# Moving sixteen conditioning loads out of a state-space stage and into the weight ring of the feed-forward product

## The chip, the cores and the metric

The kernel runs on one core of one Trainium2 chip. The metric is the device time of one execution in microseconds (us); for the kernel before the change the median of three runs is 3346.17 us (3345.36 to 3350.89). The engines of the core are TensorE (PE in the profile, its weight loads PEld), VectorE (DVE), ScalarE (ACT), GpSimd (POOL) and SyncE (SP, which here only issues transfers). Everything is 32-bit floating point.

## The reference, cut to what matters

A transformer-like stack on 256 tokens of 2048 channels. The first block mixes tokens with a state-space model (S5) whose input is modulated by a conditioning vector, gates the result with a product of 2048 x 4096 (GLU), and then runs an MLP of 2048 x 8192 x 2048 with a squared ReLU. Only the last six lines matter here:

```
sh1, sc1, gt1, sh2, sc2, gt2 = split(silu(c) @ w_mod + b_mod, 6)     # w_mod: 2048 x 12288
h     = rmsnorm(x) * (1 + sc1) + sh1;   y = s5(h) -> GLU
x     = x + gt1 * rmsnorm(y)
h     = rmsnorm(x) * (1 + sc2) + sh2
x     = x + gt2 * rmsnorm(relu(h @ w_mlp_in)**2 @ w_mlp_out)         # gt2 is needed only here
```

The six vectors of 2048 cost a read of 100 MB of `w_mod`, of which each number is used once (the context's own shift and scale come from the same columns). `gt2` is the second branch's gate. After this block come a second block with convolution, spatial gating and two gated FFNs, which the change doesn't touch.

## The kernel before, in words

**Units and the ring.** Every big matrix passes through `raw`, four slots of 1 MB (`[128, 4, 512]` each: four tiles of 128 rows by 512 columns). One such slot is a unit, four units (one slot each) are a block of 512 output columns. In the products of the later stages ACT rounds a unit to fp32r into `w_hi` (`split_unit`, L764), DVE takes the rest `w_lo = raw - w_hi` (L1014, which counts `lo_ready`), SP loads the slot again as soon as `lo_ready` says that its unit is split (L386), and PE multiplies `w_hi` with 512 columns (high and low part of the activations side by side) and `w_lo` with 256 (L478, L479). A block gathers in four of the eight PSUM banks, in turn the lower (`half` 0, banks 0 to 3) and the upper four. DVE folds the halves of a finished block together (L1020, which counts `folded`) after the splits of the next block, and a block may start when the block two before it is folded.

**The conditioning.** `w_mod` passes through the same slots in the state-space stage. There a unit is not split: PE takes it as it lies, 4 matmuls with a stationary tile of 32 columns cut from `cond`, four column groups at a time (`ada_rows`, L1601), and counts `ada_unit`. Of the 24 blocks (96 units) eight hold the first branch's shift and scale (`MOD`, blocks 0 to 3, 6, 8, 10, 12 in loading order) and are needed while the stage runs; the other sixteen (`ADA`) hold gt1, sh2, sc2 and gt2 and are turned into columns once, at the stage's end (`ada_columns`). The stage must be done with all of them before its last step, since DVE then adds the bias (`ada_done`), and the GLU's weights need the slots.

**The state-space stage** is a pipeline over 16 channel tiles, one round each, counted k = -1 to 15. PE's round k begins with the lag blocks of tile k+1 (L1660), then its states (L1676), the outputs of tile k (L1690, L1693), two units of an ADA block, small products for tiles k+2 and k+3 (L1626, L1592, L1634), output transposes (L1703), half the transposes of tile k+2 (L1647), the block's other two units, the other half of the transposes, and in rounds 0 to 3 all four units of one MOD block. Tile k+1's lag blocks wait for powers of C that POOL makes (`powers_of_c`, L2254, `cpow`; `phases` writes `pt` in between), for ACT's copies, and its outputs for a trip of the lag rows through memory (`rw` to `r_scratch` to `tw`, issued by SP). ACT issues most of the `w_mod` transfers (L1491 in `ada_units`), each after a wait until PE has used what lay in the slot; they stand in ACT's queue between its copies.

**The order** of all this is written out by hand: five instruction streams, one per engine, with semaphores between them. No scheduler moves anything.

The lines that the change and the prediction's steps touch: `block_` of GEMM_PE (a block of the products), `unit`/`block_` of GEMM_SP (SP's loads), `split` and `hidden` of GEMM_ACT, `up`/`down` of GEMM_DVE, and the three loops over k.

## Time and profile before

| what | value |
|---|---|
| median of three runs | 3346.17 us (3345.36 to 3350.89) |
| the profiled execution, its own time | 3354.33 us |
| its span on the core | 3352.5 us |
| mean granted TensorE clock | 0.967 of 2.4 GHz |
| state-space stage, up to the first matmul of the GLU | 469.4 us |
| one block of the MLP's product (four units) | 22.19 us |

The profiled execution is one run of the same program. A span is what lies between its first and last instruction; the 1.8 us around it belong to no engine. "Busy" adds up durations of an engine's instructions. A timeline row is a group of like instructions in a row on one engine: its start, its length, the line of the kernel, what it writes and reads, how many, and in brackets how long the engine had been idle before and for whom it waited. fp32 matmuls are recorded twice each, so "x16" of L1601 are 8 matmuls, which are two units. A windows row gives for each engine the busy time in a stretch, the granted clock (PEclk, 1.00 is 2.4 GHz), the busy share of the 16 DMA engines and the rate.

### The profile page before, as it was taken

What the parts mean: (1) busy time and instruction counts of PE and PEld (TensorE: products, weight loads), DVE (VectorE), ACT (ScalarE), POOL (GpSimd) and SP (SyncE); (2) the same over time, 40 slices, a digit from 0 to 9 for tenths busy, and PEclk for the clock granted to TensorE, in tenths of its full rate; (3) what the DMA queues carried; (4) which work ended last, traced back from release to release, by engine and by line L of the source; (5) the groups of instructions that cost most, each with busy time, mean ns of one, the idle gap of its engine ahead of it and who ended that gap; (6) DMA issues with size and microseconds to landing.
All of it is one profiled execution on the core that took longest, in us unless ns stands there. A gap on an engine that the chain in (4) does not pass through costs nothing.

```text
span 3352.5 us, 54116 instructions
## 1 busy us (share of the span) xinstructions
PE 3161.3 (94%) x22461; PEld 2758.8 (82%) x22461; DVE 2139.8 (64%) x1890; ACT 1431.0 (43%) x1559; POOL 324.8 (10%) x227
## 2 busy tenths in 40 slices
PE   5777789899999999899799999999989999999998
PEld 3445568888888888899798888888989888888888
DVE  7668755775555656879666655666555666566565
ACT  4446644433333334376344434433334443443343
POOL 2978730000000000000000000000000000000000
PEclk7789989999999999999899999999999999999999
DMA  9998885555555565465155565555535555556552
GB/s 296 289 306 244 254 276 179 164 164 188 188 188 188 190 191 178 144 201 194 64 182 186 185 200 189 190 192 180 197 111 169 192 191 191 189 178 205 190 188 88
DMA packets 351053, 643.59 MB, mean 192 GB/s; under 512 B 21599, under 2 KB 50359, under 8 KB 350519
## 3 DMA queue, kind: packets, MB, share of 16 engines
q1 hardware_dynamic: 309952, 561.42, 51.6%
q10 hardware_dynamic: 40951, 79.98, 7.2%
q8 instruction: 116, 1.90, 0.2%
q14 instruction: 34, 0.28, 0.0%
HBM read 637.29 MB, written 4.06 MB: 191 GB/s over the span
## 4 chain that ended last, share of the span: by engine, by line
PE 85%; DVE 5%; DMA 4%; ACT 3%; issue 1%; POOL 1%; SPq 1%; ACTq 0%; DVEq 0%; POOLq 0%
PE acc L478 42%; PE acc L479 26%; PE acc L475 5%; PE acc L476 5%; DMA raw<-in_w_mod_dram 3%; PE acc L1601 1%; ACT u L1855 1%; PE acc L1693 1%; PE acc L1676 1%; POOL cpow L2254 1%; DVE w_lo L1014 1%; DMA r_scratch<-rw 1%; DMA tw<-r_scratch 1%; DVE hf L1136 0%; PE acc L1660 0%
## 5 line engine op out<-in xcount | busy, mean ns | idle before, releaser
L1014 DVE TENSOR_TENSOR w_lo<-raw,w_hi 128x2048 fp32r<-128x2048 f32 x484 | 1105.0, 2292 | 908.3 <-ACT w_hi L764 906.6
L764 ACT ACTIVATE w_hi<-raw 128x2048 fp32r<-128x2048 f32 x484 | 923.3, 1914 | 1093.6 <-PE acc L479 1093.3
L478 PE MATMUL acc<-hid,w_hi 128*128 128x512 f32 x3776 | 1309.9, 392 | 0.0
L479 PE MATMUL acc<-xin,w_lo 128*128 128x256 f32 x3968 | 1115.3, 281 | 0.0
L479 PE MATMUL acc<-hid,w_lo 128*128 128x256 f32 x3840 | 1075.0, 280 | 0.0
L478 PE MATMUL acc<-xin,w_hi 128*128 128x512 f32 x2496 | 872.3, 394 | 6.6 <-DVE xin L1126 6.6
L478 PEld LDWEIGHTS acc<-hid,w_hi 128*128 128x128 f32 x3776 | 709.1, 188 | 156.0
L479 PEld LDWEIGHTS acc<-xin,w_lo 128*128 128x128 f32 x3968 | 750.2, 189 | 0.0
L479 PEld LDWEIGHTS acc<-hid,w_lo 128*128 128x128 f32 x3840 | 721.3, 188 | 0.1
L478 PEld LDWEIGHTS acc<-xin,w_hi 128*128 128x128 f32 x2496 | 471.6, 189 | 111.8 <-DVE xin L1126 5.3
L475 PE MATMUL acc<-xin,w_hi 128*128 128x256 f32 x1472 | 415.0, 282 | 4.1 <-DVE xin L1128 2.2
L476 PE MATMUL acc<-xin,w_hi 128*128 128x256 f32 x1472 | 413.9, 281 | 0.0
L475 PEld LDWEIGHTS acc<-xin,w_hi 128*128 128x128 f32 x1472 | 278.8, 189 | 5.9 <-issue 3.2
L476 PEld LDWEIGHTS acc<-xin,w_hi 128*128 128x128 f32 x1472 | 278.7, 189 | 0.0
L1020 DVE TENSOR_REDUCE tmp<-acc 128x1024 f32<-128x2048 f32 x98 | 223.8, 2284 | 0.0
L1601 PE MATMUL acc<-raw,cond 128*32 128x512 f32 x768 | 116.3, 714 | 53.1 <-DMA raw<-in_w_mod_dram 51.1
L1601 PEld LDWEIGHTS acc<-raw,cond 128*32 128x32 f32 x768 | 20.7, 121 | 115.8 <-DMA raw<-in_w_mod_dram 80.0
L838 ACT ACTIVATE xin<-tmp 128x1024 f32 x22 | 23.3, 1060 | 158.0 <-DVE tmp L1266 158.0
L2254 POOL TENSOR_TENSOR cpow<-cpow,ptmp 128x1024 f32<-128x1024 f32 x32 | 75.6, 2362 | 1.3
L1855 ACT ACTIVATE u<-acc,modt 128x32 f32<-128x32 f32 x256 | 70.6, 414 | 1.0 <-PE acc L1634 0.6
L1476 POOL MEMSET conv_in<- 128x120 f32 x1 | 0.2, 203 | 727.6 <-DVE xr L1114 727.6
L2254 POOL TENSOR_TENSOR ptmp<-ct,lpc 128x1024 f32<-128x1024 f32 x32 | 61.9, 1934 | 76.7 <-ACT ct L1793 55.5
(306 smaller groups left out, 2171.1 us busy)
## 6 DMA issues: line engine op xcount, KB each, us to landing
raw<-in_ffn_w_gate_dram SPq DMA_DIRECT2D x88, 1024.0 KB, 5.2
raw<-in_ffn_w_up_dram SPq DMA_DIRECT2D x88, 1024.0 KB, 5.2
raw<-in_ffn_w_down_dram SPq DMA_DIRECT2D x88, 1024.0 KB, 5.2
raw<-in_w_mod_dram ACTq DMA_DIRECT2D x76, 1024.0 KB, 10.1
raw<-in_w_mlp_in_dram SPq DMA_DIRECT2D x64, 1024.0 KB, 5.3
raw<-in_w_mlp_out_dram SPq DMA_DIRECT2D x64, 1024.0 KB, 5.2
raw<-in_s_w_glu_dram SPq DMA_DIRECT2D x32, 1024.0 KB, 5.4
raw<-in_ab_w_in_dram SPq DMA_DIRECT2D x32, 1024.0 KB, 5.5
```

Source lines behind the costliest of these rows:

```text
L475: pe.matmul(bank[:, 0:TOK], w_hi[:, slot, w], operand[:, kt, 0:TOK], start=first, stop=False)
L476: pe.matmul(bank[:, 0:TOK], w_hi[:, slot, w], operand[:, kt, TOK:2 * TOK], start=False, stop=False)
L478: pe.matmul(bank, w_hi[:, slot, w], operand[:, kt, :], start=first, stop=False)
L479: ins = pe.matmul(bank[:, 0:TOK], w_lo[:, slot, w], operand[:, kt, 0:TOK], start=False, stop=last)
L764: act.activation(w_hi[:, slot, :], raw[:, slot, :, :].rearrange("p k n -> p (k n)"), ACT.Copy).then_inc(hi_ready, 1)
L1014: dve.tensor_tensor(w_lo[:, slot, :], raw[:, slot, :, :].rearrange("p k n -> p (k n)"), w_hi[:, slot, :].bitcast(F32), SUB).then_inc(lo_re ...
L1020: dve.tensor_reduce(dst, acc[:, 4 * half:4 * half + 4, :].rearrange("p a (t b) -> p a b t", t=2), AX.X, ADD).then_inc(folded, 1)
L1601: ins = pe.matmul(ps[0][32 * q:32 * q + 32, :], cond[:, kk * UK + q, window:window + 32], raw[:, kk, q, :], start=(m + kk == 0), stop=(kk ...
L1676: ins = pe.matmul(ps[1 + ri][s * NST:(s + 1) * NST, cb * 64:(cb + 1) * 64], ew[:, ri, cb, s * NST:(s + 1) * NST], uv[:, :, ::-1] if d else ...
L1693: ins = pe.matmul(o, st[s * NST:(s + 1) * NST, ri, 4 * d + kp, :], cpow[cp][s * NST:(s + 1) * NST, ri, 4 * d + kp, :], start=False, stop=( ...
L1855: ins = act.activation(u[b][:, g, q * NCH:(q + 1) * NCH], ps[6][:, g * 64 + q * NCH:g * 64 + (q + 1) * NCH], ACT.Identity, bias=modt[:, 16 ...
L2254: return pool.tensor_tensor(o, x, y, op)
```

## The change

Four of the sixteen ADA blocks (gt2, 16 units, 16.8 MB) no longer pass through `raw` in the state-space stage. They pass through the ring in the first part of the MLP, one after every second block of its first eight. Stage by stage:

- State-space stage: 20 blocks instead of 24. MOD blocks are now 0 to 6 and 8 in loading order. The ADA blocks are PE's work in rounds 3 to 14 (12 of them) and no longer in rounds -1 to 14 (16). So round -1 has no unit, rounds 0 to 2 have the four of a MOD block, round 3 has eight (ADA and MOD), rounds 4 to 14 have four as before.
- SP: after the eight loads of an even and an odd block of the MLP come four loads of `w_mod` (`late_gate`), each waiting for the split of the odd block's unit in its slot. The loads of the next block wait until PE has used the late units (`ada_unit`).
- PE: in an odd block, after its first unit, the late units 0 and 1, and after its second the units 2 and 3 (`late_rows`, 32 columns of `ada` broadcast as the stationary tile, into bank 0); after the third unit four small matmuls that turn the row into columns (`late_columns`). Before the first late unit PE waits for the fold of the block before, since bank 0 belongs to it.
- ACT: two small copies per late block, between the splits of the next block (`split_and_turn`).
- DVE: the gate's bias and norm weight are applied in two small instructions in the last part of the MLP.
- The first eight blocks of the MLP are written out and no longer part of a loop on PE and SP; the last three of four parts remain loops.

```diff
-        MOD = [(0, 1), (2, 3), (6, 8), (10, 12)]
-        ADA = [4, 5, 7, 9, 11] + list(range(13, 24))
+        MOD = [(0, 1), (2, 3), (4, 5), (6, 8)]
+        ADA = [7] + list(range(9, 20))
+        ADA_ROUND = 3
...
-                if k + 1 < KT:
-                    if k in (-1, 2, 4):
-                        pe.wait_ge(ada_sb, {-1: 2, 2: 3, 4: 4}[k])
-                    ada_rows(ADA[k + 1], 15 - (k + 1), (0, 1))
+                if k in (-1, 2, 4):
+                    pe.wait_ge(ada_sb, {-1: 2, 2: 3, 4: 4}[k])
+                if ADA_ROUND <= k < KT - 1:
+                    ada_rows(ADA[k - ADA_ROUND], 15 - (k - ADA_ROUND), (0, 1))
...
+            def late_gate(i, u):
+                for k in range(UK):
+                    sp.wait_ge(lo_ready, u + k + 1)
+                    sp.dma_start(raw[:, k, :, :], w_mod[:, k * UK:(k + 1) * UK, 2 * D + (KT - LATE + i) * UN:2 * D + (KT - LATE + i + 1) * UN]
+                                 ).then_inc(raw_ready[k], 16)
...
-            with sp.Fori(0, MLP_PARTS) as q:
+            for c in range(2 * NCK):
+                block_(MLP[0] + 4 * c, *((w_in, c * UN, 0) if c < NCK else (w_out, (c - NCK) * UN, 0)), late=c // 2)
+                if c % 2:
+                    late_gate(c // 2, MLP[0] + 4 * c)
+            with sp.Fori(1, MLP_PARTS) as q:
...
+                    if late is not None and k < 2:
+                        if k == 0:
+                            pe.wait_ge(folded, blk)
+                        late_rows(late, blk - MLP[1], (2 * k, 2 * k + 1))
+                    if late is not None and k == 2:
+                        late_columns(late)
...
+            def late_rows(i, c, units):
+                for kk in units:
+                    pe.wait_ge(raw_ready[kk], 16 * (ADA_UNITS // SLOTS + MLP[0] // SLOTS + c + 1 + i + 1))
+                    for q in range(UK):
+                        kt = KT * 3 + kk * UK + q
+                        ins = pe.matmul(ps[0][32 * q:32 * q + 32, :], ada[:, kt:kt + 1].broadcast_to([P, 32]), raw[:, kk, q, :],
+                                        start=(kk == 0), stop=(kk == UK - 1), skip_group_check=True)
+                    ins.then_inc(ada_unit, 1)
+
+            def late_columns(i):
+                pe.wait_ge(ada_sb, 5 + i + 1)
+                for r in range(NT):
+                    ins = pe.matmul(ps[1][:, r:r + 1], rs[:, r // 2, r % 2 * P:(r % 2 + 1) * P], one_of_32, start=True, stop=True)
+                ins.then_inc(ada_col, 1)
...
+            def split_and_turn(grp, i):
+
+                split(grp, slots=(0, 1), late=i + 1)
+                act.wait_ge(ada_unit, ADA_UNITS + 4 * (i + 1))
+                act.activation(rs[:, :, :].rearrange("p a t -> p (a t)"), ps[0], ACT.Copy).then_inc(ada_sb, 1)
+                split(grp, slots=(2,), late=i + 1)
+                act.wait_ge(ada_col, 5 + i + 1)
+                act.activation(coef[:, 2 * KT + NT * i:2 * KT + NT * (i + 1)], ps[1][:, 0:NT], ACT.Copy).then_inc(ada_done, 1)
+                split(grp, slots=(3,), late=i + 1)
...
+            dve.wait_ge(ada_done, 1 + LATE)
+            x_step(dve.tensor_tensor(gate, gate, par[:, 3 * KT:4 * KT], ADD))
+            x_step.settle()
+            x_step(dve.tensor_tensor(gate, gate, par[:, cols["mlp_post"]:cols["mlp_post"] + KT], MUL))
+            x_step.settle()
```

**PE, round 1 of the state-space stage.** The end of round 1, from the last outputs of tile 1 to the first lag blocks of tile 3, in the kernel before (matmuls counted once each here; `cpow` carries a buffer number):

```order
L1693 MATMUL acc<-cpow_64,st 32x128 x16
L1601 MATMUL acc<-raw,cond 32x512 x8
L1626 MATMUL acc<-mrhs,s5c 128x32
L1592 MATMUL acc<-s5c,craw 64x64 x8
L1634 MATMUL acc<-consts,xt 128x64 x8
L1703 MATMUL acc<-s5c,zt 128x32 x8
L1647 MATMUL acc<-consts,bpow 128x128 x8
L1601 MATMUL acc<-raw,cond 32x512 x8
L1647 MATMUL acc<-consts,bpow 128x128 x8
L1601 MATMUL acc<-raw,cond 32x512 x16
L1660 MATMUL acc<-cpow_63,bd 32x128 x16
```

The same stretch after the change (L1662 is `ada_rows`, L1708 the transposes, L1721 the lag blocks):

```order
L1754 MATMUL acc<-cpow_64,st 32x128 x16
L1687 MATMUL acc<-mrhs,s5c 128x32
L1653 MATMUL acc<-s5c,craw 64x64 x8
L1695 MATMUL acc<-consts,xt 128x64 x8
L1764 MATMUL acc<-s5c,zt 128x32 x8
L1708 MATMUL acc<-consts,bpow 128x128 x16
L1662 MATMUL acc<-raw,cond 32x512 x16
L1721 MATMUL acc<-cpow_63,bd 32x128 x16
```

Both pairs of units in the middle of the round are gone; the four units of the MOD block stay at its end.

**PE, the MLP's second block.** The seam between its first and second unit after the change (with the semaphores that an instruction waits for):

```order
L492 MATMUL acc<-xin,w_hi 128x512
L493 MATMUL acc<-xin,w_lo 128x256
L512 MATMUL acc<-raw,ada 32x512 [waits raw_ready0,folded]
L512 MATMUL acc<-raw,ada 32x512 x3
L512 MATMUL acc<-raw,ada 32x512 [waits raw_ready1]
L512 MATMUL acc<-raw,ada 32x512 x3
L492 MATMUL acc<-xin,w_hi 128x512 [waits lo_ready,xin_ready]
L493 MATMUL acc<-xin,w_lo 128x256
```

Before, the pair L478, L479 of the first unit was followed at once by the first pair of the second; now two late units and a wait for `folded` stand between.

**SP, the loads of the MLP's first part** after the change (before, they were two loops of `w_mlp_in` and `w_mlp_out` loads alone, each waiting for `lo_ready`):

```order
L390 DMA raw<-in_w_mlp_in_dram 128x4x512 [waits lo_ready] x8
L399 DMA raw<-in_w_mod_dram 128x4x512 [waits lo_ready] x4
L390 DMA raw<-in_w_mlp_in_dram 128x4x512 [waits lo_ready,ada_unit] x8
L399 DMA raw<-in_w_mod_dram 128x4x512 [waits lo_ready] x4
L390 DMA raw<-in_w_mlp_out_dram 128x4x512 [waits lo_ready,ada_unit] x8
```

Each set of four late loads sits between blocks, and the loads behind it in SP's queue now also wait for PE's late matmuls.

## Rows read from the trace of the kernel before

**Rows 1.** The page: PE and DMA in 40 slices of 83.8 us (tenths).
```profile
PE   5777789899999999899799999999989999999998
DMA  9998885555555565465155565555535555556552
```

**Rows 2.** Windows: rounds 0 to 3, rounds 4 to 13, one MLP block.
```profile
core 0: us, PE busy (x) PEld busy (x) DVE busy (x) ACT busy (x) POOL busy (x), PEclk, DMA share, GB/s
767.19:789.38 22.19, 22.19 (x130) 19.54 (x129) 13.78 (x7) 8.62 (x5) 0.00 (x0) 1.00 0.57 190
...
109.42:141.95 32.53, 23.16 (x298) 12.72 (x302) 18.37 (x35) 13.63 (x40) 31.66 (x25) 0.77 0.96 281
141.95:170.51 28.56, 23.63 (x302) 12.97 (x298) 16.60 (x32) 13.07 (x40) 28.10 (x20) 0.80 0.94 314
170.51:202.58 32.07, 23.37 (x310) 12.76 (x306) 16.61 (x32) 13.64 (x42) 31.39 (x21) 0.82 0.99 331
202.58:232.28 29.70, 22.16 (x302) 12.46 (x298) 17.18 (x36) 13.07 (x40) 21.71 (x15) 0.84 0.89 287
232.28:442.06 209.78, 165.83 (x2656) 113.51 (x2648) 169.54 (x324) 128.05 (x392) 163.93 (x103) 0.93 0.86 255
```

**Rows 3.** Timeline of PE: starts of rounds 0, 2 and what ended round 1.
```profile
109.42 1.35 PE L1660 MATMUL acc<-cpow,bd 128*32 128x128 f32 x32 [4.35 <-POOL cpow L2254]
...
163.09 1.07 PE L1601 MATMUL acc<-raw,cond 128*32 128x512 f32 x8 [2.23 <-DMA raw<-in_w_mod_dram]
165.86 1.94 PE L1601 MATMUL acc<-raw,cond 128*32 128x512 f32 x8 [1.70 <-DMA raw<-in_w_mod_dram]
168.80 1.93 PE L1601 MATMUL acc<-raw,cond 128*32 128x512 f32 x8 [1.01 <-DMA raw<-in_w_mod_dram]
170.51 1.55 PE L1660 MATMUL acc<-cpow,bd 128*32 128x128 f32 x32
```

**Rows 4.** Timeline of POOL: the last powers for tiles 1, 2, 3, 4.
```profile
107.02 2.34 POOL L2254 TENSOR_TENSOR cpow<-cpow,ptmp 128x1024 f32<-128x1024 f32 x1
...
138.73 2.35 POOL L2254 TENSOR_TENSOR cpow<-cpow,ptmp 128x1024 f32<-128x1024 f32 x1
...
158.00 2.37 POOL L2254 TENSOR_TENSOR cpow<-cpow,ptmp 128x1024 f32<-128x1024 f32 x1
...
177.29 2.38 POOL L2254 TENSOR_TENSOR cpow<-cpow,ptmp 128x1024 f32<-128x1024 f32 x1
```

**Rows 5.** Timeline of PE in a round at full clock, and round 11's start and end.
```profile
179.24 1.06 PE L1612 MATMUL acc<-s5c,adarow 128*128 128x4 f32 x8
180.16 0.39 PE L1626 MATMUL acc<-mrhs,s5c 128*128 128x32 f32 x2
...
305.34 1.92 PE L1601 MATMUL acc<-raw,cond 128*32 128x512 f32 x16
307.19 0.41 PE L1626 MATMUL acc<-mrhs,s5c 128*128 128x32 f32 x2
...
360.45 1.08 PE L1660 MATMUL acc<-cpow,bd 128*32 128x128 f32 x32 [1.57 <-ACT acc L1816]
...
378.77 1.08 PE L1660 MATMUL acc<-cpow,bd 128*32 128x128 f32 x32 [1.62 <-ACT acc L1816]
```

**Rows 6.** Timeline of ACT in the MLP: splits that wait for the end of a unit.
```profile
789.53 1.92 ACT L764 ACTIVATE w_hi<-raw 128x2048 fp32r<-128x2048 f32 x1 [3.69 <-PE acc L479]
795.02 1.92 ACT L764 ACTIVATE w_hi<-raw 128x2048 fp32r<-128x2048 f32 x1 [3.57 <-PE acc L479]
```

**Rows 7.** Timeline of DVE there: the last split of a block, then the fold.
```profile
791.48 2.29 DVE L1014 TENSOR_TENSOR w_lo<-raw,w_hi 128x2048 fp32r<-128x2048 f32 x1 [3.31 <-ACT w_hi L764]
793.69 2.28 DVE L1020 TENSOR_REDUCE tmp<-acc 128x1024 f32<-128x2048 f32 x1
```

**Rows 8.** The page, DMA issues: KB each, median us from issue to landing.
```profile
raw<-in_w_mod_dram ACTq DMA_DIRECT2D x76, 1024.0 KB, 10.1
raw<-in_w_mlp_in_dram SPq DMA_DIRECT2D x64, 1024.0 KB, 5.3
```

More of the change, by code:

```diff
@@ L53, in main_consts @@
     c[:, 2 * P + 7] = 1.0
+    c[::32, 2 * P + 15] = 1.0
     return c
@@ L380, in GEMM_SP, with unit @@
         def GEMM_SP(sp):
-            def unit(u, slot, src, k, col, early=None):
+            def unit(u, slot, src, k, col, early=None, late=0):
+                if late:
+                    sp.wait_ge(ada_unit, ADA_UNITS + 4 * (late - 1) + slot + 1)
                 if early is not None and early < SLOTS:
@@ L404, in GEMM_SP @@
                 glu(i)
-            with sp.Fori(0, MLP_PARTS) as q:
+            for c in range(2 * NCK):
[3 more added lines that the diff above has]
+            with sp.Fori(1, MLP_PARTS) as q:
                 with sp.Fori(0, 4) as i:
-                    block_(32 * q + (4 * i + MLP[0]), w_in, q * (4 * UN) + i * UN)
+                    block_(32 * q + (4 * i + MLP[0]), w_in, q * (4 * UN) + i * UN, late=LATE)
                 with sp.Fori(0, 4) as i:
@@ L455, in GEMM_PE, with block_ @@
         def GEMM_PE(pe):
-            def block_(u, blk, half, operand, ready=None, units=4, slot0=0, between=None, after=1, order=None, narrow=False, piece=None):
+            def block_(u, blk, half, operand, ready=None, units=4, slot0=0, between=None, after=1, order=None, narrow=False, piece=None, late=None):
                 if not isinstance(blk, int):
@@ L704, in down @@
                         block_(32 * q + (8 * i + (MLP[0] + 16 + 4 * j)), 8 * q + (2 * i + (MLP[1] + 4 + j)), j, hid, hid_from(4 * q))
-            for c in range(NCK):
-                block_(MLP[0] + 4 * c, MLP[1] + c, c % 2, xin, normed_from(0), piece=first_from(0) if c == 0 else None)
-            down(0)
+            for c in range(2 * NCK):
+                if c and c % 2 == 0:
+                    pe.wait_ge(ada_done, 1 + c // 2)
+                block_(MLP[0] + 4 * c, MLP[1] + c, c % 2, *((xin, normed_from(0)) if c < NCK else (hid, hid_from(0))),
+                       piece=first_from(0) if c == 0 else None, late=c // 2 if c % 2 else None)
+            pe.wait_ge(ada_done, 1 + LATE)
             with pe.Fori(1, MLP_PARTS - 1) as q:
@@ L766, in GEMM_ACT, with split @@
             ADA_DMA = ADA_UNITS // SLOTS
-            def split(grp, early=False, slots=range(SLOTS)):
+            def split(grp, early=False, slots=range(SLOTS), late=LATE):
                 for slot in slots:
-                    split_unit(4 * grp + slot, slot, 16 * grp + 16 * (ADA_DMA + 1), early)
+                    split_unit(4 * grp + slot, slot, 16 * grp + 16 * (ADA_DMA + late + 1), early)
+            def split_and_turn(grp, i):
[6 more added lines that the diff above has]
+                split(grp, slots=(3,), late=i + 1)
             def weigh(n, c):
@@ L794, in seam @@
                     for grp in left:
-                        split(grp, slots=(SLOTS - 1,))
+                        split(grp, slots=(SLOTS - 1,), late=LATE * s.n)
                     act.wait_ge(x_ms, s.n + 1)
@@ L882, in GEMM_ACT @@
                 for g in (2 * i + 1, 2 * i + 2):
-                    split(g, slots=(0, 1) if g < 8 else (0,))
+                    split(g, slots=(0, 1) if g < 8 else (0,), late=0)
                     if g in (3, 4):
@@ L890, in GEMM_ACT @@
                         weigh(0, 0)
-                        split(g, slots=(2,))
+                        split(g, slots=(2,), late=0)
                         weigh(0, 1)
-                        split(g, slots=(3,))
+                        split(g, slots=(3,), late=0)
                         break
                     if g < 8:
-                        split(g, slots=(2, 3))
+                        split(g, slots=(2, 3), late=0)
                 if i < 3:
@@ L900, in GEMM_ACT @@
             weigh(0, NCK - 2)
-            split(8, slots=(0, 1, 2))
+            split(8, slots=(0, 1, 2), late=0)
             act.wait_ge(pe_unit, 32)
@@ L912, in up @@
                         hidden(4 * q + (2 * i + j), 2 * i + j, j, hid)
-            with act.Fori(0, MLP_PARTS - 1) as q:
+            for c in range(2 * NCK):
+                if c % 2:
+                    split_and_turn(G + 1 + c, c // 2)
+                else:
+                    split(G + 1 + c, late=c // 2)
+                if c < NCK:
+                    hidden(c, c, c % 2, hid)
+            with act.Fori(1, MLP_PARTS - 1) as q:
                 up(q)
@@ L1358, in GEMM_DVE @@
             up(MLP_PARTS - 1)
+            gate = coef[:, 2 * KT:3 * KT]
+            dve.wait_ge(ada_done, 1 + LATE)
[3 more added lines that the diff above has]
+            x_step.settle()
             down(MLP_PARTS - 1, 0, 0)
@@ L1933, in _ @@
                     copy_e(k + 2)
[L1934 removed]
+                if ADA_ROUND <= k < KT - 2:
+                    ada_units(act, ADA[k - ADA_ROUND] + 1, (2, 3))
                 if k + 3 < KT:
```

30 lines of the change are left out of this document (16 added, 14 removed).

## The prediction

> **What bounds the kernel now.** I read the page's slices first. From the seventh slice on PE is busy nine tenths or more in nearly every slice and the DMA engines are at about half; in the first six PE has gaps and the DMA engines stand at eight or nine tenths [rows 1]. So the change takes transfers from where they are scarce and puts them where there is room, but it also takes PE work from where PE has gaps and puts it where PE has none. The time is the difference of two terms, and each needs its own reading.
>
> Next I cut the state-space stage into rounds, from one start of the lag blocks to the next [rows 2]. Rounds 0 to 3, with eight units each, take 32.53, 28.56, 32.07 and 29.70 us at a DMA share of 0.89 to 0.99. Rounds 4 to 13, with four units, take 209.78 / 10 = 20.98 us each at 0.86. The reader is to see that four more units cost about 9 us per round, and that only rounds -1 to 3 can change: from round 4 on the same four units per round stand at the same place in the new program.
>
> Then I asked which wait ends last in each early round. In round 1 PE comes to the four MOD units and waits for three of them one after the other (2.23, 1.70, 1.01 us idle), and right behind them the next lag blocks start without a wait [rows 3]: the loads set the end. But round 0 starts on POOL (PE idle 4.35 us for `cpow`), so POOL is a second clock beside the loads. Its powers for tile 1 end at 107.02 + 2.34 = 109.36, for tile 2 at 141.08, for tile 3 at 160.37, for tile 4 at 179.67 [rows 4]; POOL has no gap between (busy 31.66 of 32.53 and 28.10 of 28.56 us [rows 2]). These are times before which the lag blocks of tiles 2, 3 and 4 cannot start, whatever the loads do.
>
> **The state-space term.** Round -1 loses four units, but its end waits for POOL at 109.36 before and after, and what POOL works from (tables and first modulation) comes from blocks 0 and 1, which are loaded as before: 0 gained. If that cover went, PE's 3.7 us for these units would come free.
>
> Round 0: from 8 to 4 units, but tile 2's powers end at 141.08, and its lag blocks started at 141.95. Gained 0.87 us. That is the step most easily overlooked: this round of 32.53 us was bound twice, and POOL's one-time scaling of powers lies in it.
>
> Rounds 1 and 2: four units each, like a later round. Two floors: POOL makes a tile in 19.29 us (160.37 - 141.08), and the best later round takes 378.77 - 360.45 = 18.32 us [rows 5]. The average is 20.98 us at a granted clock of 0.93 [rows 2], with its dips and late lag rows in it. The MOD units stand at the round's end in one piece (two pairs of 1.85 us), behind both halves of the transposes, so PE can no longer fill its wait for ACT's copies in the middle; on the other hand the first pair no longer delays the small products. I see no reason for better or worse than the average and take 20.9: lag blocks of tile 4 at 141.1 + 41.8 = 182.9, against 202.58. Floor: 179.7 by POOL. Upper bound: the rounds stay at 24 us (the slowest later ones), 189.1.
>
> Round 3 has eight units, as before: 29.70 us then; the three rounds not tied to POOL average 30.1. I take 29.8, from 28.6 to 32.1. Tile 5's lag blocks at 212.7 against 232.28: gained 19.6 us, and between 232.28 - (189.1 + 32.1) = 11 and 232.28 - (179.7 + 28.6) = 24. POOL, 8 us ahead or more by then, is not late in round 4: tile 6 is ready at 179.67 + 2 x 19.29 = 218.3, wanted at 233. The later rounds keep their length, so the gain reaches the GLU. At the stage's end DVE has a shorter add and one 16-column copy more: 0, give or take 0.2.
>
> **The MLP term.** PE is busy 22.19 of 22.19 us in a block at clock 1.00, a unit is 5.55 us [rows 2], so what PE gets there is paid in full.
>
> Late units: in the state-space stage at full clock two units take 307.19 - 305.34 = 1.85 us until the next matmul starts [rows 5], same stationary width, same 512 columns. Four gates of two such pairs: 8 x 1.85 = 14.8 us.
>
> Columns: four matmuls of the same size but 4 columns took 180.16 - 179.24 = 0.92 us [rows 5]; four gates: 3.7 us.
>
> The wait for the fold: bank 0 is free when the block before is folded. DVE folds after the last split: a unit ends at 789.5 (ACT's split starts on it) and the next at 795.0 [rows 6]; the fold runs from 793.69 to 795.97 [rows 7]. PE comes to the late units at 795.0 and waits 0.95 us, 1.05 with the hand-over. This holds in the up and the down blocks alike, since both fold after four splits: 4 x 1.05 = 4.2 us. Behind the waiting matmul PE's whole product is queued. It could be 0 if DVE were early, 2.3 (a whole fold) if something held DVE.
>
> Switching: 16 changes between the 128-wide and the 32-wide tiles. In the trace the next matmul starts 0.07 us before the 32-wide group's recorded end. I take nothing beyond the 1.85. Upper bound: one matmul of 0.39 us drained at each, 6.2 us. The Trainium skill, "TensorEngine Tiling (Array Packing)", section Key Properties, says that changing the tiling mode drains TensorE. The trace neither shows such a cost as a gap nor excludes that it lies inside the 1.85; by that rule read at its dearest the term would be the upper bound, and the time 6 us above my forecast.
>
> The ring: between the use of a late unit and the split of the next block's unit in that slot there must be time to load. Slot 0 is free about 2 us after the odd block's first unit, lands 5.3 us later [rows 8] (8 to 10 if crowded), is split for 4.2 us (1.92 on ACT, 2.29 on DVE), and is wanted three units, 16.6 us and more, after that first unit: 4 to 9 us of room. Slot 2 frees some 10 us after it and is wanted two units later than slot 0: the same. In a late block eight units pass in about 28 us; a ring block shows a share of 0.57 for four in 22.19 us, 3.2 us each, so 25 of 28 us. Tight, not over. Cost 0; if the cover is gone, a unit (5.5 us) per gate.
>
> ACT gets 0.6 + 0.2 us per gate in idle time of 3.6 us per unit, DVE two tiny instructions in the last part within 3.3 us of idle time: 0. SP's waits: 0. Sixteen fewer issues on ACT in the state-space stage are in its rounds already.
>
> Sum: 14.8 + 3.7 + 4.2 = 22.7, and 0.3 for the semaphores inside: +23.0, from 18.5 (no fold wait) to 29.5 (drain).
>
> **The sum.** -19.6 + 23.0 = +3.4 us. Against the profiled execution, 3354.33 + 3.4 = 3357.7; that execution was 8.2 us above the median, so for the median 3346.17 + 3.4 = 3349.6. A difference under 0.2% (6.7 us) can't be told from none.
>
> **Rivals.**
>
> *Faster: all early rounds fall, round 0 and 3 too.* Mechanism: POOL's 141.08 is itself late only because its inputs or its memory accesses are held up by the crowded transfers, and the lighter traffic shortens round 3. Then four rounds give 30.7 - 20.98 = 9.7 us each, 39 us less the eight-unit round that remains (9): 30 us. Time 3346.2 - 30 + 23 = 3339. For it: share 0.96 in round 0. Against: POOL's instructions last the same in crowded and light rounds (2.34 to 2.38 us) and it had no idle time. It decides if tile 2's lag blocks start before 139.
>
> *Slower: rounds 1 and 2 don't fall.* The MOD block's four loads are issued by ACT when PE has used the block before, at the end of a round, and are wanted at the end of the next; with the trip of the lag rows through memory they could keep a round at 25 us. Gain 20 - 2 x 4 = 11 or less, cost 23 to 25: +13, 3359. For it: loads need 10.1 us to land under traffic [rows 8]. Against: they have a whole round. It decides if these rounds are over 24 us.
>
> *Slower: the ring starves behind the late units.* Each gate costs one unit more: +3.4 + 22 = +25, 3372. For it: 25 of 28 us. Against: the slack above. It would show as PE idle for `lo_ready` in the MLP's blocks 2, 4, 6, 8.
>
> *The drain is paid*: +3.4 + 6.2, 3356.
>
> **Chances.** Forecast (within -3 and +9, 3343 to 3355) 0.56; faster rival 0.15; rounds stay 0.14; ring 0.06; drain 0.09. The range leaves out the ring and half the dearest and cheapest cases: 3337 to 3361. Faster by over 0.2%: 0.16 (the rival and the forecast's best edge). Slower by over 0.2%: the two slower rivals, half the drain's, and a little of the forecast's upper edge, 0.27. The same: 0.57.
>
> **What would show it.** Lag blocks of tile 1 at 109.4 again, of tile 2 at 141.1 on a POOL wait; rounds 1 and 2 at 20 to 22 us, round 3 at 29 to 31; GLU's first matmul at about 450. In the MLP, odd blocks of the first part at 22.19 + 5.7 = 27.9 us with PE idle 1 us before the late matmuls for DVE's fold, even blocks at 22.2; two late units at 1.85 us. It is wrong if round 0 shortens by more than 2 us, if an odd block costs over 7 us more, or if an even block is longer.

## The result and the profile after

| kernel | median | spread, runs |
|---|---|---|
| before, beside it | 3348.66 us | 3340.09 to 3353.72, 20 |
| after | 3359.44 us | 3348.78 to 3363.76, 20 |

The ratio is 1.0034, with a 95% interval from 1.0027 to 1.0041: the change costs about 11 us. The forecast was +3.4. The profiled executions differ by less, 3354.33 and 3359.15 us; why is shown with the second profiles of both. Medians below leave out one execution of the kernel with all four late units behind the second unit, which took 11031.7 us at a mean granted clock of 0.339.

The page after, against [rows 1] (40 slices of 83.9 us, in tenths):

```profile
PE   5688789899999999999799999999989999999998
DMA  9588975376656565465255565555534555556552
```

The reader is to see the second slice: DMA falls from 9 to 5 there. In the ninth to eleventh, where the late units now are, it stands at 7, 6 and 6, where it was 5.

Windows of the kernel after: rounds 0 to 3, rounds 4 to 13, an odd and an even block of the MLP's first part. They answer to [rows 2].

```profile
core 0: us, PE busy (x) PEld busy (x) DVE busy (x) ACT busy (x) POOL busy (x), PEclk, DMA share, GB/s
108.96:140.65 31.69, 20.89 (x267) 14.70 (x267) 19.00 (x35) 13.19 (x40) 30.90 (x24) 0.72 0.46 141
140.65:164.98 24.33, 21.02 (x266) 14.48 (x270) 16.60 (x32) 12.57 (x39) 23.87 (x17) 0.67 0.33 94
164.98:186.11 21.13, 19.72 (x278) 14.23 (x274) 16.61 (x32) 13.76 (x42) 20.67 (x15) 0.76 0.80 240
186.11:218.34 32.23, 23.08 (x302) 12.42 (x298) 22.37 (x36) 13.48 (x40) 31.55 (x19) 0.84 0.99 307
218.34:422.94 204.60, 163.31 (x2656) 113.05 (x2648) 168.88 (x324) 127.93 (x392) 169.80 (x108) 0.93 0.89 264
683.59:711.90 28.31, 27.27 (x170) 21.24 (x169) 13.83 (x9) 9.26 (x7) 0.00 (x0) 1.00 0.92 328
711.90:734.08 22.18, 22.18 (x130) 19.52 (x129) 13.81 (x8) 8.62 (x5) 0.00 (x0) 1.00 0.57 190
```

Two things stand here. The DMA engines are at 0.46 and 0.33 in rounds 0 and 1, and at 0.99 in round 3: the loads are spread unevenly. And an odd block is 6.12 us longer than an even one (28.31 against 22.19), although DMA is at 0.92 only and the clock is full.

What sets the early rounds, on PE's timeline; it answers to [rows 3]:

```profile
140.65 1.93 PE L1721 MATMUL acc<-cpow,bd 128*32 128x128 f32 x32 [8.93 <-POOL cpow L2319]
...
157.65 1.94 PE L1708 MATMUL acc<-consts,bpow 128*128 128x128 f32 x8 [2.52 <-ACT ew L1887]
159.52 5.64 PE L1662 MATMUL acc<-raw,cond 128*32 128x512 f32 x32
...
201.90 1.97 PE L1708 MATMUL acc<-consts,bpow 128*128 128x128 f32 x8 [3.60 <-DVE bpow L2015]
...
213.93 1.14 PE L1662 MATMUL acc<-raw,cond 128*32 128x512 f32 x8 [2.48 <-DMA raw<-in_w_mod_dram]
216.64 1.93 PE L1662 MATMUL acc<-raw,cond 128*32 128x512 f32 x8 [1.57 <-DMA raw<-in_w_mod_dram]
```

Round 0 ends with PE idle 8.93 us for POOL's powers; in round 1 no load is waited for, but the four MOD units take 5.64 us, where two pairs at full clock take 2 x 1.85 = 3.7 [rows 5]; of rounds 0 to 3 only round 3 still waits for `w_mod`.

The late units of the MLP's second block (PE) and the folds around it (DVE; [rows 7] before):

```profile
684.60 0.28 PE L493 MATMUL acc<-xin,w_lo 128*128 128x256 f32 x1
685.93 1.92 PE L512 MATMUL acc<-raw,ada 128*32 128x512 f32 x16 [1.04 <-DVE tmp L1075]
687.78 0.50 PE L492 MATMUL acc<-xin,w_hi 128*128 128x512 f32 x1
...
693.32 0.28 PE L493 MATMUL acc<-xin,w_lo 128*128 128x256 f32 x1
693.53 1.92 PE L512 MATMUL acc<-raw,ada 128*32 128x512 f32 x16
695.38 0.50 PE L492 MATMUL acc<-xin,w_hi 128*128 128x512 f32 x1
...
701.03 0.95 PE L519 MATMUL acc<-consts,rs 128*128 128x1 f32 x8
701.85 0.48 PE L492 MATMUL acc<-xin,w_hi 128*128 128x512 f32 x1
```
```profile
683.59 2.28 DVE L1075 TENSOR_REDUCE tmp<-acc 128x1024 f32<-128x2048 f32 x1
...
711.90 2.28 DVE L1075 TENSOR_REDUCE tmp<-acc 128x1024 f32<-128x2048 f32 x1
```

The folds of the two blocks start 28.31 us apart. In steady work a w_lo matmul starts 0.12 us before the next w_hi one. So the first late group starts 685.93 - 684.72 = 1.21 us late, the two groups take 1.85 each, the columns 0.82, and the rest of the 6.12, 0.4 us, lies in small pieces at the switches (0.50 or 0.48 us for the first w_hi matmul behind each group instead of 0.39, and 0.09 us ahead of the second late group).

### The profile page after: what moved, and what is told of

It is laid out like the page before. It is cut to its first block, busy times and chain, and to the rows that moved or that the text cites. A ratio compares the mean times of both kernels' runs of the same rounds, so it can differ in the third digit from the quotient of the medians.

```text
span 3357.2 us, 54092 instructions
## 1 busy us (share of the span) xinstructions
PE 3166.6 (94%) x22493; PEld 2768.6 (82%) x22493; DVE 2145.3 (64%) x1892; ACT 1434.5 (43%) x1567; POOL 324.7 (10%) x227
## 4 chain that ended last, share of the span: by engine, by line
PE 84%; DVE 5%; DMA 3%; ACT 3%; POOL 2%; issue 2%; SPq 1%; ACTq 0%; DVEq 0%; POOLq 0%
PE acc L492 42%; PE acc L493 26%; PE acc L489 5%; PE acc L490 5%; DMA raw<-in_w_mod_dram 1%; PE acc L1662 1%; POOL cpow L2319 1%; DMA tw<-r_scratch 1%; DMA r_scratch<-rw 1%; ACT u L1916 1%; PE acc L1754 1%; POOL ptmp L2319 1%; ACT w_hi L802 1%; DVE w_lo L1069 1%; DVE tmp L1075 1%
## 5 line engine op out<-in xcount | busy, mean ns | idle before, releaser
L1662 PE MATMUL acc<-raw,cond 128*32 128x512 f32 x640 | 94.3, 712 | 27.4 <-DMA raw<-in_w_mod_dram 27.4
L886 ACT ACTIVATE xin<-tmp 128x1024 f32 x22 | 23.3, 1061 | 158.0 <-DVE tmp L1321 158.0
L1662 PEld LDWEIGHTS acc<-raw,cond 128*32 128x32 f32 x640 | 18.4, 124 | 79.2 <-DMA raw<-in_w_mod_dram 42.2
L900 ACT ACTIVATE tmp<-tmp 128x1024 f32<-128x1024 f32 x22 | 23.3, 1061 | 107.2 <-DVE tmp L1314 107.2
```

Source lines behind the costliest of these rows:

```text
L886: act.activation(dst[:, ds(CH * chunk, CH) if not isinstance(chunk, int) else slice(CH * chunk, CH * (chunk + 1)), 0:TOK], tmp[:, half], A ...
L1662: ins = pe.matmul(ps[0][32 * q:32 * q + 32, :], cond[:, kk * UK + q, window:window + 32], raw[:, kk, q, :], start=(m + kk == 0), stop=(kk ...
```

## The experiments

What had to be told apart: is the miss in the stage (less gained than the 19.6 us of the forecast), in the MLP (a late block costs more than 5.75 us), or was the execution profiled before a poor base? And within each part, what sets the price?

**The stage's part alone.** The second branch's gate is taken from its bias alone; its sixteen units are neither loaded nor multiplied anywhere.

```diff
-        ADA_UNITS, LATE = 32 + 3 * KT, KT // 4
+        ADA_UNITS, LATE = 32 + 3 * KT, 0
...
-                    late_gate(c // 2, MLP[0] + 4 * c)
...
-            x_step(dve.tensor_tensor(gate, gate, par[:, 3 * KT:4 * KT], ADD))
+            x_step(dve.tensor_tensor(gate, par[:, 2 * KT:3 * KT], par[:, 3 * KT:4 * KT], ADD))
```

> The changed kernel without any late unit: no loads, no late matmuls, no waits for them in the MLP (left out of the computation: the second branch's gate, 16 units of w_mod). It is the state-space part of the change alone. Theory A (the two terms as the profiles of the pair show them: the stage gives 18 to 21 us, four gates take 24.5): 3348.7 - 19 = about 3330, and the first matmul of the GLU at 451. Theory B (the profiled execution of the changed kernel was a lucky one: the stage gives only 12 to 14 us in the median, which is where the 10.8 us between the medians come from and not the 4.7 between the profiles): 3335 to 3337. Theory C (the MLP's part costs over 30 us in the median): 3330, and the difference sits in the next run.

Measured: 3332.28 us against 3347.38, ratio 0.9961 (0.9948 to 0.9975): 13 us less by the ratio, 15 by the medians, and 8 to 17 by the interval; not 20.

**The MLP's part alone.** The tables and loops of the stage as before, with all 24 blocks there, and the late units besides: the gate's columns are loaded and multiplied twice.

```diff
-        ADA_UNITS, LATE = 32 + 3 * KT, KT // 4
+        ADA_UNITS, LATE = 32 + 4 * KT, KT // 4
...
-        MOD = [(0, 1), (2, 3), (4, 5), (6, 8)]
-        ADA = [7] + list(range(9, 20))
-        ADA_ROUND = 3
+        MOD = [(0, 1), (2, 3), (6, 8), (10, 12)]
+        ADA = [4, 5, 7, 9, 11] + list(range(13, 24))
+        ADA_ROUND = -1
...
-                    ada_units(act, (5, 6, 7, 9)[k])
+                    ada_units(act, ADA[k + 1] + 2)
```

> The state-space stage of the kernel before with all 24 blocks, and besides the 16 late units in the MLP as after the change (the gate's 16 units are loaded and multiplied twice). It is the MLP part alone. Theory A: each of four gates costs 6.12 us as in the profile of the changed kernel, 24.5 in all: 3373, with odd blocks of 28.3 us and even ones of 22.2. Theory B: the same, since B puts the missing microseconds in the state-space stage. Theory C: over 30 us, 3379 or more.

Measured: 3373.83 us, ratio 1.0081 (1.0068 to 1.0094): 26 to 27 us more, with an interval from 23 to 31. Its odd blocks take 28.31 us. The medians of the two halves add up, -15.1 + 26.4 = +11.3, which is near the change (+10.8). So nothing speaks for the halves acting on each other; a few us of it would hide in intervals this wide.

**All four late units behind the second unit**, where the fold is long done:

```diff
-                    if late is not None and k < 2:
-                        if k == 0:
-                            pe.wait_ge(folded, blk)
-                        late_rows(late, blk - MLP[1], (2 * k, 2 * k + 1))
+                    if late is not None and k == 1:
+                        pe.wait_ge(folded, blk)
+                        late_rows(late, blk - MLP[1], (0, 1, 2, 3))
```

> The changed kernel with all four late units of a gate behind the odd block's second unit, none behind the first: bank 0 has then long been folded, and PE changes between wide and 32-wide tiles twice per gate and no longer four times. Theory A1 (the wait for the fold is 1.05 us per gate, a change of tile width costs nothing): a late block of 28.31 - 1.05 = 27.26 us, 4.2 us less than the changed kernel. Theory A2 (the 0.45 us per gate over my sum is the change of width, 0.11 per switch): 27.0 us, 5.1 less. Theory D (the ring needs the early start; later loads make ACT's splits late): a block not shorter than 28.3 us or a longer even block.

Measured: 3371.5 us, ratio 1.0068 (1.0055 to 1.0081), 12 us slower than the changed kernel. Of the theories only D is left: it named the cause, later loads that make ACT's splits late, but no size. The wait for the fold did go; a dearer one came. PE and ACT in its second block of the MLP:

```profile
691.65 3.64 PE L511 MATMUL acc<-raw,ada 128*32 128x512 f32 x32
...
703.56 1.72 PE L518 MATMUL acc<-consts,rs 128*128 128x1 f32 x8 [2.53 <-ACT rs L814]
705.14 0.77 PE L492 MATMUL acc<-xin,w_hi 128*128 128x512 f32 x1
705.71 0.41 PE L493 MATMUL acc<-xin,w_lo 128*128 128x256 f32 x1
```
```profile
698.42 1.91 ACT L801 ACTIVATE w_hi<-raw 128x2048 fp32r<-128x2048 f32 x1 [8.89 <-DMA raw<-in_w_mlp_in_dram]
701.11 1.91 ACT L801 ACTIVATE w_hi<-raw 128x2048 fp32r<-128x2048 f32 x1 [0.78 <-DMA raw<-in_w_mlp_in_dram]
702.93 0.58 ACT L814 ACTIVATE rs<-acc 128x512 f32<-128x512 f32 x1
```
```profile
core 0: us, PE busy (x) PEld busy (x) DVE busy (x) ACT busy (x) POOL busy (x), PEclk, DMA share, GB/s
705.14:710.41 5.27, 5.27 (x18) 4.49 (x19) 2.50 (x2) 0.67 (x2) 0.00 (x0) 0.50 1.05 386
710.41:717.00 6.59, 6.59 (x39) 5.81 (x39) 1.53 (x1) 1.92 (x1) 0.00 (x0) 0.99 0.52 188
```

Read them backwards. PE idles 2.53 us ahead of the column matmuls because ACT's copy of the row (702.93) stands in ACT's queue behind the splits of the next block's first two units; those wait 8.89 us for their loads; and the loads can't start until PE has used the late units in these slots, which is now 10.3 us behind the fold's start (695.22 - 684.88) instead of 4.2 (687.78 - 683.59) for slots 0 and 1. After that idle time the granted clock is 0.50 (1.2 GHz) for 5.3 us, in which the pairs of w_hi and w_lo matmuls start 0.64 us apart instead of 0.35. The other three late blocks wait 2.07, 2.76 and 3.06 us at this place and are followed by 0.50 to 0.56. Late blocks are 32.80, 32.37, 32.88 and 32.82 us instead of 28.31. In the changed kernel the same copy starts at 697.80, 3.2 us ahead of its use (701.03).

**Narrower late units.** All 64 matmuls stay (128 in the records), but each takes 64 of the 512 columns, so the gate is computed only in part.

```diff
-                        ins = pe.matmul(ps[0][32 * q:32 * q + 32, :], ada[:, kt:kt + 1].broadcast_to([P, 32]), raw[:, kk, q, :],
+                        ins = pe.matmul(ps[0][32 * q:32 * q + 32, 0:64], ada[:, kt:kt + 1].broadcast_to([P, 32]), raw[:, kk, q, 0:64],
```

> The changed kernel with the late matmuls over 64 of the 512 columns (left out: seven eighths of the gate's product; the loads, waits and number of instructions are the same). Theory A (a late unit costs what PE streams, 1.85 us per two units): rows shrink to the weight loads, about 0.1 us per recorded matmul at most, so two units take 0.5 to 1.7 us; if columns rule, a late block is about 25 us and the kernel 11 to 13 us faster than the changed one. Theory E (the weight loads rule, 105 ns for each of 16): two units stay at 1.7 us or more and the time stays within 2 us. Theory D (the ring is what costs): the block stays at 28.3 us with PE idle.

Measured: 3346.09 us, 13 us less than the changed kernel, with odd blocks of 25.32 us. PE's row:

```profile
683.77 0.43 PE L512 MATMUL acc<-raw,ada 128*32 128x64 f32 x16 [1.05 <-DVE tmp L1075]
684.13 0.50 PE L492 MATMUL acc<-xin,w_hi 128*128 128x512 f32 x1
```

The group takes 0.36 us to the next start instead of 1.85, with an eighth of the columns. So 4 x 2 x 1.49 = 11.9 us of the MLP's price are the seven eighths of the columns that are left out here, and 3.13 us per gate stay without them (the wait, the column matmuls, the switches, and 0.72 of the groups).

**No round of eight units.** The first ADA block goes back to round -1, and rounds 0 to 3 keep four units each:

```diff
-        MOD = [(0, 1), (2, 3), (4, 5), (6, 8)]
-        ADA = [7] + list(range(9, 20))
-        ADA_ROUND = 3
+        MOD = [(0, 1), (2, 3), (5, 6), (7, 8)]
+        ADA = [4] + list(range(9, 20))
+        ADA_AT = {-1: 0, **{k: k - 3 for k in range(4, 15)}}
...
-                    ada_units(act, (5, 6, 7, 9)[k])
+                    ada_units(act, (6, 7, 8, 9)[k])
```

> The changed kernel with the conditioning blocks dealt out anew: the MOD pairs are (0,1), (2,3), (5,6), (7,8), the first ADA block (4) is consumed in round -1, and the others from round 4 on, so that no round has eight units. If round 3 is long because eight units of 1 MB pass in it (PE waits there for loads of w_mod three times, 5.5 us in all, at a DMA share of 0.98), it falls from 32.2 to about 21 us, round -1 stays at 22 us (its end is set by POOL's powers at 109), and the time falls by 8 to 11 us against the changed kernel: near 3350. The rival theory is that round 3 is long for another reason (DVE's powers of b, for which PE waits 3.6 us, or the lag rows' way through memory); then it stays above 27 us and the time within 4 us of the changed kernel.

Measured: 3349.08 us, 10.4 less than the changed kernel (10 by the ratios). Round 3 takes 21.2 us, and a wait of 2.54 us for `bpow` is still in it: DVE didn't set round 3, the eight units did. Of the 11.0 us that it lost, about half were waits for loads (0.84, 0.65, 2.48 and 1.57 us in the changed kernel) and about half the ADA block's own matmuls (0.99, 0.99 and 3.57 us there).

**POOL's scaling moved**, in the kernel before and in the kernel after. POOL scales powers for tiles 2 to 15 in round 0 (the ten groups on `lpc` run from 115.73 to 128.1) and earlier idles 23.77 us until ACT has copied `ct` (at 66.74):

```diff
             scale_powers(c, 0, 2 * CB)
+            scale_powers(c, 2 * CB, NCB)
...
             pool.wait_ge(phase_done, 2)
-            scale_powers(c, 2 * CB, NCB)
```

> The kernel before, with POOL's scaling of the powers for tiles 2 to 15 (about 12.4 us of POOL's time in round 0) moved up into a stretch in which POOL idles for the first modulation. If round 0 is bound twice there, by POOL and by the loads of eight units, tile 2's powers come 12 us earlier and the lag blocks of tile 2 hardly move: round 0 stays at 28 to 32 us and the time within 0 to 4 us of the kernel before. If POOL alone set round 0, it falls to about 21 us and the time by about 10 us.

> The changed kernel with the same move of POOL's scaling. By my theory round 0 has only POOL left as its bound (PE waits 8.9 us for the powers there), so it falls from 31.7 to 20 to 24 us; and since PE no longer idles before round 1, its clock there is higher than 0.67 and round 1 falls from 24.3 to about 21. Together 8 to 14 us less than the changed kernel, near 3348, if rounds 2 and 3 keep their length. The rival is that the transfers set the later rounds: then round 3, with eight units, grows by what rounds 0 and 1 lose, and the time stays within 4 us of the changed kernel.

Measured: the kernel before stays, 3347.36 us (ratio 1.0003, 0.9992 to 1.0013). The changed one goes to 3346.60 us (0.9995, 0.9986 to 1.0003 of the kernel before), 12.8 less than without. What PE waits for in round 0 of the kernel before with the scaling moved, and rounds 0 to 3 of the changed one with it:

```profile
131.46 1.61 PE L1601 MATMUL acc<-raw,cond 128*32 128x512 f32 x8 [2.40 <-DMA raw<-in_w_mod_dram]
134.17 1.94 PE L1601 MATMUL acc<-raw,cond 128*32 128x512 f32 x8 [1.10 <-DMA raw<-in_w_mod_dram]
```
```profile
core 0: us, PE busy (x) PEld busy (x) DVE busy (x) ACT busy (x) POOL busy (x), PEclk, DMA share, GB/s
108.50:131.10 22.60, 20.74 (x270) 14.81 (x274) 18.99 (x35) 12.59 (x39) 21.78 (x15) 0.70 0.22 54
131.10:151.50 20.40, 16.33 (x270) 11.00 (x266) 16.60 (x32) 13.20 (x40) 20.02 (x14) 0.92 0.84 258
151.50:172.00 20.50, 17.15 (x278) 11.89 (x274) 16.60 (x32) 13.77 (x42) 20.12 (x14) 0.92 0.82 258
172.00:202.30 30.30, 22.51 (x302) 12.11 (x298) 21.73 (x36) 13.49 (x40) 29.76 (x19) 0.86 1.03 329
```

Round 0 was bound twice, as the prediction had it: with eight units the loads hold it at 28.9 us (tile 2's lag blocks start at 138.87) when POOL is done at 129.6, with four it falls to 22.6. And round 1 falls from 24.3 to 20.4 with PE's clock at 0.92 instead of 0.67: the same work (266 to 270 records), 21.0 us of PE before and 16.3 now.

**The first late pair a quarter of a unit later**, so that the fold is done, without moving the loads by much:

```diff
                     for q in range(UK):
+                        if late is not None and (k, q) == (1, 1):
+                            pe.wait_ge(folded, blk)
+                            late_rows(late, blk - MLP[1], (0, 1))
...
-                    if late is not None and k < 2:
-                        if k == 0:
-                            pe.wait_ge(folded, blk)
-                        late_rows(late, blk - MLP[1], (2 * k, 2 * k + 1))
+                    if late is not None and k == 1:
+                        late_rows(late, blk - MLP[1], (2, 3))
```

> The changed kernel with the first two late units a quarter of a unit later: PE multiplies the first quarter (1.4 us) of the block's second unit before it waits for the fold, instead of waiting right behind the first unit. If the 1.0 us idle before the first late pair is only the wait for DVE's fold, it goes, and a late block falls from 28.3 to about 27.2 us, so the time by about 4 us. The rival, from the run with all four late units behind the second unit: any delay of the late units delays the next block's loads into the same slots, ACT's splits of them, and behind those its copy of the late rows, for which PE waits. There PE's delay was 5.6 us against 2.6 us of slack; here it is 0.4 us net, so I expect no wait at the column matmuls. If there is one over 1 us, late blocks are 29 us and more.

Measured: 3352.13 us, ratio 1.0017 (1.0007 to 1.0028). PE is busy without a gap in the late block:

```profile
679.92:707.12 27.20, 27.20 (x170) 21.25 (x169) 13.83 (x9) 9.27 (x7) 0.00 (x0) 1.00 0.93 316
```

The blocks give 4 x 1.11 = 4.4 us; the ratios of the two kernels differ by 0.0017, 5.7 us, and their medians by 7.3. PE is done with slots 0 and 1 4.5 us behind the fold's start (684.39 - 679.92), only 0.3 later than in the changed kernel, and the copy of the row is again in time.

**The three repairs together.**

> The changed kernel with three edits at once: no round of eight units, POOL's scaling moved into its idle time, and the first late pair a quarter of a unit later. Against the changed kernel they saved 10, 13 and 6 to 7 us one by one. If they act at different places (round 3, rounds 0 and 1, the MLP's late blocks), they add up to about 29 us: near 3330, some 15 us less than the kernel before. The rival is that the first two draw on the same thing: with POOL's work moved, the loads of rounds 0 to 3 all come earlier, round -1 has a fifth block of loads again, and the stage is bound by its transfers; then one of the two gains is lost and the time is 3338 to 3343.

Measured: 3337.02 us (3327.63 to 3338.51), ratio 0.9958 (0.9941 to 0.9974): 10.8 us less than the kernel before by the medians and 14 by the ratio, and 22 or 25 less than the changed kernel. Its early rounds:

```profile
108.10:130.40 22.30, 19.23 (x266) 13.40 (x270) 18.99 (x35) 13.55 (x40) 21.52 (x15) 0.78 0.63 168
130.40:150.90 20.50, 16.43 (x274) 11.09 (x270) 16.60 (x32) 13.21 (x40) 20.12 (x14) 0.92 0.82 257
150.90:172.00 21.10, 20.29 (x278) 15.19 (x274) 16.60 (x32) 13.82 (x42) 20.72 (x15) 0.76 0.79 244
172.00:195.30 23.30, 18.88 (x274) 13.00 (x270) 21.34 (x36) 13.51 (x40) 22.84 (x15) 0.78 0.73 235
```

The median lies where the rival had it, but its mechanism is not there: neither of the two stage repairs is lost. Tile 5's lag blocks start at 195.3, against 202.3 and 206.3 with one of them and 214 to 218 with none. The gains by the medians, 10.4, 12.8 and 7.3, add up to 30 where 22 came; by the ratios they are 10.0, 13.1 and 5.7, 29 where 25 came. Each ratio is known to 3 or 4 us and that of the repaired kernel to 5 or 6, so this does not show that anything was lost. The profiles show nothing lost either: at the MLP's first fold the two stage repairs gain 7 and 9 us one by one and 16.6 together, against the middle of the six profiles in the table below that have neither (681.9).

**Both kernels profiled again.**

> The kernel before once more, for a second profile. Theory: the execution profiled first was a slow one in rounds 4 to 14 (209.8 us, where five changed kernels with the same program there took 202.4 to 205.8) and at the GLU's start; so rounds 0 to 3 are again 122 to 124 us in all, but rounds 4 to 14 near 205 and the first fold of the MLP's block 1 near 701 instead of 704.95. Rival: the stage's later rounds really are faster in all changed kernels; then it is 209 to 210 again.

> The changed kernel once more. Rounds 0 to 3 near 31.7, 24.3, 21.1 and 32 us as in its first profile, and an odd block of the MLP's first part at 28.3 us. If the stage gains 14 us and the MLP costs 26, the two second profiles differ by 9 to 13 us.

Measured: 3345.0 and 3356.2 us, 11.2 apart. Lengths by the starts of the lag blocks and DVE's folds, in us:

| | round 0 | 1 | 2 | 3 | 4 to 13 | tile 5's lag blocks at | first MLP fold at | odd block |
|---|---|---|---|---|---|---|---|---|
| before | 32.5 | 28.6 | 32.1 | 29.7 | 209.8 | 232.3 | 704.95 | 22.19 |
| before, again | 32.2 | 28.4 | 31.2 | 31.3 | 202.8 | 232.2 | 696.28 | 22.19 |
| MLP's part alone | 33.2 | 28.7 | 30.2 | 30.7 | 205.6 | 232.6 | 701.34 | 28.31 |
| stage's part alone | 31.7 | 24.0 | 21.0 | 30.0 | 205.8 | 215.5 | 682.43 | 22.19 |
| after | 31.7 | 24.3 | 21.1 | 32.2 | 204.6 | 218.3 | 683.59 | 28.31 |
| after, again | 31.7 | 23.0 | 20.5 | 30.9 | 203.7 | 214.2 | 681.12 | 28.31 |
| after, late units narrow | 31.7 | 23.6 | 21.0 | 31.3 | 202.4 | 215.2 | 681.43 | 25.32 |
| all four behind the second unit | 31.7 | 22.8 | 20.5 | 32.4 | 205.8 | 215.9 | 684.88 | 32.80 |
| first pair later | 31.7 | 22.5 | 20.5 | 32.2 | 202.3 | 214.6 | 679.92 | 27.20 |
| after, scaling moved | 22.5 | 20.4 | 20.5 | 30.3 | 207.2 | 202.3 | 672.95 | 28.31 |
| no round of eight | 31.7 | 23.1 | 21.6 | 21.2 | 206.9 | 206.3 | 675.13 | 28.31 |
| three repairs | 22.3 | 20.5 | 21.1 | 23.3 | 206.2 | 195.3 | 665.31 | 27.20 |
| before, scaling moved | 28.9 | 30.1 | 29.3 | 30.9 | 206.8 | 229.2 | 695.69 | 22.19 |

The first theory on the base holds: the execution on which the forecast stood lost 7 us in rounds 4 to 13, in which PE's units are the same before and after, and was 8.7 us late at the MLP's first fold against the second one of the same program.

Another 1.6 us of the 8.7 lie behind the last wait of the seam between GLU and MLP, and they are clock. From the first matmul behind this wait of 2.54 us to the first fold, in the first and in the second profile of the kernel before:

```profile
693.30:704.95 11.65, 11.65 (x58) 10.17 (x59) 8.91 (x5) 5.56 (x4) 0.00 (x0) 0.85 0.66 203
686.21:696.28 10.07, 10.07 (x58) 8.87 (x59) 8.90 (x4) 5.57 (x4) 0.00 (x0) 1.00 0.65 198
```

The work and the wait are the same, the granted clock is not. Of the thirteen profiles four have 10.07 us and a clock of 1.00 here, the other nine 11.46 to 11.65 us and 0.85 to 0.87, kernels with and without late units among both.

## Why the prediction was right or wrong

The time lay in the range, 1.6 us inside its slower end (3361), and outside the 3343 to 3355 that stood for the forecast itself. It fell on the number of a rival, 3359 for early rounds that don't fall, whose mechanism did not come: that is luck, and so is part of the hit. The forecast was 9.8 us too low; 2.5 of them are the kernel before, whose median is 3348.66 over 20 runs and was 3346.17 over three. The other 7 are in the sum of +3.4.

The second profiles of both kernels show where such a difference lies, though one pair of executions can't say how much of each piece is the change. Their spans differ by 3354.2 - 3343.2 = 11.0 us. The stage is 18.0 us ahead at tile 5's lag blocks and the MLP's first fold 15.2 us; of the 2.8 us between, 1.6 are the clock at the seam, 0.9 rounds 4 to 13, and the rest small pieces. The late blocks cost 24.5, and what follows them is 1.7 us longer. Against 19.6 and 23.0 that is 4.4, 1.5 and 1.7 us, the 7.6 that the sum was too low.

**Round -1 and round 0: right.** Tile 1's lag blocks start at 108.96 for POOL (109.42 before), tile 2's at 140.65 (forecast 141.1), and the two runs with POOL's scaling moved show that this round has the two bounds that were named. The faster rival, which needed a start before 139, is out.

**Rounds 1 and 2: the mechanism right, round 1 mis-sized.** Round 2 takes 20.5 to 21.1 us in six profiles (forecast 20.9). Round 1 takes 22.5 to 24.3 in the same six, 23.3 in the middle, 2.4 us over the forecast. The step that failed is "I see no reason for better or worse than the average". There was one: PE stands idle 8.9 us ahead of the round, and then works through it at a clock of 0.67, partly at the low level of 1.2 GHz, so that it is busy for 21.0 us with what takes 16.3 at 0.92. The units that went away had kept PE going in round 0 (busy 23.16 us at a clock of 0.77 in [rows 2], 20.89 at 0.72 now), and none of its waits there was over 3.8 us. The rival in which these rounds stay over 24 us for the loads' sake is out: round 1 of the first profile meets its sign (24.33), but nothing waits for a load there.

**Round 3: mis-sized.** Forecast 29.8, measured 30.0 to 32.4 us, 31.8 in the middle. It has to bring in eight units at a DMA share near 1, after rounds in which the DMA engines stand at 0.33 to 0.80. That would fit ACT's issuing of loads by the round; no run issues them earlier, so this is not shown. Without the eight-unit round the kernel is 10 us faster.

**The stage's term: 19.6 forecast, 13 to 18 measured.** At tile 5's lag blocks the six profiles with the new stage and POOL's scaling in place lie at 214.2 to 218.3, 215.4 in the middle, against 232.2 to 232.6: 17 us gained. Rounds 1 and 3 took back 2.4 and 2.0 of the forecast, and tile 1's lag blocks start about 1 us earlier. The stage's part alone says 13 to 15, with an interval from 8 to 17. In the first pair of profiles the stage seemed to gain 19.1 us at tile 15 (442.06 to 422.94), as forecast, and that was luck: 5 of them lie in rounds 4 to 13.

**The MLP's term: 23.0 forecast, 24.5 in the profiles, 26 to 27 (23 to 31) by the run.** The four late blocks cost 4 x 6.12 = 24.5 us in every profile with this order. By the terms: late units 14.8 forecast and 14.8 measured, and the narrow run shows that columns rule them; columns 3.7 against 3.3; the fold wait 4.2 against 4.8, and its cause is shown by the run that takes it away; the switches 0 against 1.6. The Trainium skill, "TensorEngine Tiling (Array Packing)", Key Properties, has TensorE drained at each such change of mode. The pieces above, about 0.1 us at a switch, would fit that, but at a quarter of the dearest reading. They don't prove it: the first w_hi matmul behind the column matmuls, which are 128 wide, is recorded at 0.48 us too, without a change of mode. (The recorded upper bound of the term, 29.5, should read 23.0 + 6.2 = 29.2.) The ring rival falls too: the even blocks stay at 22.18 us, and PE never waits for `lo_ready` between the late units. The rest up to 26 is not in the late blocks. From the MLP's ninth fold to the end of the span the four profiles without late units took 2469.4 to 2470.3 us and the nine with them 2468.6 to 2472.8, and the MLP's part alone, from which the 26 comes, 2469.8. The seam from the GLU (the last GLU fold to the MLP's first) takes 64.0 or 65.4 to 65.6 us by execution, in kernels with and without the change alike, and nearly all of the difference is the clock behind its last wait. With an interval from 23 to 31 the run does not contradict 24.5.

**The ring: right, but thinner than the even blocks show.** The forecast gave 4 to 9 us of room and looked at PE's wait for `lo_ready` only. The room that ran out first, when slots 0 and 1 came free 6.1 us later, was that of ACT's copy behind the splits.

## What to carry to other kernels

Loads taken from a stage pay only where loads were its last wait: list for each stretch the second bound, and ask also what PE's clock does when the work that filled its wait is gone. On an engine that runs at full clock without gaps, a moved unit costs what its matmuls stream plus every wait on its path, and it must stand where both the wait ahead of it and the slot behind it have room: here releasing the first two slots 0.3 us later was right and 6.1 us later too late. Before a difference of some us is read off two profiles, profile both programs twice and compare the stretches that the change leaves alone.

## What the runs showed of the hardware

The granted clock fell behind short idle times of PE, but not each time. With all four late units behind the second unit, waits of 2.53, 2.07, 2.76 and 3.06 us were each followed by 5.1 to 5.3 us at 0.50 to 0.56, where the changed kernel with a wait of 1.04 us kept 1.00; the first such block was 4.5 us longer for a wait that was 1.5 us longer. Behind the 2.54 us of the seam the clock stayed at 1.00 in four profiles of thirteen and the stretch averaged 0.85 to 0.87 in nine, at a price of 1.4 to 1.6 us, and the same program did both.

A 32-column matmul group costs by the columns that stream through: 16 records take 1.85 us at 512 columns and 0.36 at 64, so an estimated 0.15 us of the group don't depend on them, if the cost is a straight line between the two (1.85 = a + 512 b, 0.36 = a + 64 b).

Two executions of one program were 8.7 us apart at the MLP's first fold. Rounds 4 to 13 took 202.8 and 209.8 us in them: PE was busy for 161.9 and 165.8 us at a clock of 0.94 and 0.93, and idle for 40.9 and 44.0. What set this off is open.
